# Dilated attention computed two heads at a time on halves of TensorE's array, with projection blocks between the pairs

## The chip, the cores and the metric

The kernel runs on one core of a Trainium2 chip as one launch. The metric is device time in microseconds (us), the median of several runs; lower is better.

## The reference

The reference is a network of two blocks over 256 tokens of width 1024, in float32. The first block has a mixing layer with a recurrence, a gated FFN with a short convolution, a dilated attention layer with 16 heads of 64 features, and another FFN. The second block (with a modulation by a condition vector) has a block attention with 8 heads of 128 features, a gated FFN, a convolution layer and another FFN. The change concerns only the dilated attention:

```python
h = rmsnorm(x, od_norm[j])
qkv = (h @ od_w_qkv[j]).reshape(bsz, t_len, 3, C_HEADS, C_HEAD)
y = dilated_attention(qkv[:, :, 0], qkv[:, :, 1], qkv[:, :, 2])
x = x + y @ od_w_out[j]
```

`dilated_attention` runs a softmax for each of the patterns (window, dilation) = (128, 1), (512, 4), (2048, 16) and weighs the three results by their log-sum-exp. That equals one softmax over all causal keys in which a key counts as often as patterns hold it; both kernels compute it so, with log(count) added to the scores.

## The kernel before

Everything stays in SBUF; only weights stream in. A projection weight comes as chunks of 2 MB in a ring of two slots, by DMAs that SyncE (SP) issues. Each chunk is used in halves of 128 x 2048. For each half ACT writes a rounded high part (`split_hi`, line 564, tile `whi`), DVE writes the rest (`split_lo`, line 570, tile `wlo`), and PE makes three products (hi x hi, hi x lo, lo x hi) per tile. Four buffers hold the parts, and each engine's `w.go()` makes the parts three halves ahead of the one that is used. Each engine's program is written out by hand, and its instructions run in that order; they meet by semaphores. A PSUM bank's semaphore counts how often the bank was read out; `opened(e, key)` waits until the previous user of the bank has been read, and `read_out(key)` names the count at which this one has. `bank_plan` fixes which bank each product uses.

The stage of the change, in order:
- `pe_tile` makes Q and K in eight tiles (`("qkv", i, q)`, lines 993 to 995), with features on the partitions; ACT copies each tile out (line 1420). Two pairs of products of the modulation (`adahi`, `adalo`, `one_r`) stand ahead of tile 7 and behind it.
- Then a loop over i = 0 to 18. In step i PE makes the scores of head i (two products, lines 2389 and 2390: queries 0 to 127 against 128 keys, queries 128 to 255 against 256 keys), turns the exponentials of head i - 2 (three transposes, line 2373), and multiplies head i - 3 with V (lines 2405 to 2407, P as the stationary operand, 64 columns of V moving, the result with tokens on the partitions). `pe_rows` (lines 1008 to 1010) makes V in four halves within steps 0, 1, 3 and 4.
- DVE adds the bias and takes maxima (lines 1865, 1869) and copies three of four turned heads out (1877); ACT takes the exponentials (1444) and copies every fourth (1453).
- After each eight heads DVE inverts the sums and scales the result into `xn` (`od_scaled`, lines 1836 and 1841), PE turns it with eight transposes (`od_turned`, line 2382), and ACT and DVE write its high and low parts (`yhi` line 1436, `ylo` line 1849).
- `pe_sum_rows` multiplies with `od_w_out` in four blocks (line 1022, 24 products of 512 columns each); in the last two blocks the second half of the tokens waits until the first half's sums are done, so that the next norm can begin (its turn is line 759).

Elsewhere in the kernel, the first mixing layer already has float32 products on halves of the array: line 2213 (64 rows, halves alternating) and line 2292 (64 columns of the stationary operand, halves alternating). The second block's attention already scales P on DVE (line 1940) and writes its result with features on the partitions (1521 on ACT, 1947 on DVE).

Of the kernel before, what the change touches and what calls it, by code (L numbers as in the profile page):

```python
# [7 lines left out]
F32 = mybir.dt.float32  # L8
U32 = mybir.dt.uint32
F32R = mybir.dt.float32r  # L10
ALU = mybir.AluOpType
# [107 lines left out]
MOD_Q = {0: 0, 1: 1, 3: 2, 4: 3}  # L119

# [139 lines left out]
def bank_plan():  # L260
# [69 lines left out]
    for m in range(8):  # L330
        for n in ADA["qkv"]["sums", ("tile", m)]:
            P.use(("ada", n), r())
        for j in behind_norm(m):
            P.use(("qkv", j // 2, j % 2), r())
    for n in ADA["qkv"]["sums", "end"]:
        P.use(("ada", n), r())
# [11 lines left out]
    def od_between(i):  # L348
        if i in (0, 3):
            P.use(("v", "qkv", i // 3, 0), 4)  # L350
            P.use(("v", "qkv", i // 3, 1), 5)
        if i == 12:
            P.use(("yt", 0, 0), r())
            P.use(("yt", 0, 1), r())

    def od_values(h):
        if h % 8 == 0:
            for n in range(2):
                P.use(("o", n, h // 8), (6, 4)[h // 8] + n)

    attention("od", 16, od_between, od_values)
    sums("od_out", (2, 3, 6, 7))
    r = Ring((0, 1))
    P.use(("yt", 1, 0), r())
    P.use(("yt", 1, 1), r())
# [39 lines left out]
def program(nc, A, consts, out):  # L405
    with ExitStack() as ctx:
# [300 lines left out]
        YTOK = XN  # L707
        od_sums, od_rl = (ATT[:, 32 * i:32 * i + 32].rearrange("p (h n) -> p h n", n=2) for i in (1, 2))
# [510 lines left out]
        def scalar_program(e):  # L1219
# [193 lines left out]
            for i in range(4):  # L1413
                for q in range(2):
                    split_hi(e, w.go())
                    if i == q == 0:
                        act_first(e, 2)
                    e.wait_ge(*block_done(("qkv", i), q))
                    j = 4 * (i % 2) + 2 * q
                    e.activation((QT if i < 2 else KT)[:, j:j + 2, :], c3(ps_of(("qkv", i, q))[:, :], 2),  # L1420
                                 ACT.Copy).then_inc(bank_sem(("qkv", i, q)), 1)
                    act_ada_parts(e, ADA["qkv"]["parts", ("tile", 2 * i + q)], 2)

            def v_piece(name, i, q):
                split_hi(e, w.go())
                if q:
                    e.wait_ge(*used_up((name, 4 + i), 1))
                    e.wait_ge(S["ada_acc"], 4 * ADA["qkv"]["range"][1])
                    for n in range(2):
                        key = ("v", name, i, n)  # L1430
                        e.activation(VV[:, n, 512 * i:512 * i + 512], ps_of(key)[:, :], ACT.Copy).then_inc(bank_sem(key), 1)

            def od_turned(q):
                for n in range(2):
                    e.wait_ge(S["yt_turned"], 2 * q + n + 1)
                    e.activation(YT[0][:, 4 * q:4 * q + 4, 128 * n:128 * n + 128],
                                 c3(ps_of(("yt", q, n))[:, :], 4), ACT.Copy).then_inc(S["od_hi"], 1)
# [17 lines left out]
            for i in range(19):  # L1455
                if i < 16:
                    exp(i, "od", 16, 0, None)
                if i in (0, 1, 3, 4):
                    v_piece("qkv", i // 3, i % 3)
                if i == 12:  # L1460
                    od_turned(0)
                if 2 <= i < 18:
                    turned(i - 2, "od", 0)
            act_load_root(e)
            split_hi(e, w.go())
            od_turned(1)
            for i in range(3):
                split_hi(e, w.go(AHEAD * (i < 2)))
# [42 lines left out]
            for i in range(11):  # L1511
                if i < 8:
                    exp(i, "mo", 8, 32, None)
                if i < 2:
                    v_piece("qkv2", 1, i)
                if 2 <= i < 10:
                    turned(i - 2, "mo", 16)
                if i >= 3:
                    h = i - 3
                    e.wait_ge(S["at_values"], 16 + h + 1)  # L1520
# [92 lines left out]
        def vector_program(e):  # L1613
# [211 lines left out]
            for m in range(8):  # L1825
# [5 lines left out]
            dve_ada_sums(e, ADA["qkv"]["sums", "end"])  # L1831

            def od_scaled(q):
                r = od_rl[:, 8 * q:8 * q + 8, :]
                e.wait_ge(S["at_exp"], 8 * q + 8)
                e.reciprocal(r, od_sums[:, 8 * q:8 * q + 8, :]).then_inc(S["od_inverse"], 1)
                e.wait_ge(S["od_inverse"], q + 1)
                e.wait_ge(S["at_values"], 8 * q + 8)
                for n in range(2):
                    key = ("o", n, q)  # L1840
                    e.tensor_tensor(c3(YTOK[:, n, 512 * q:512 * q + 512], 8), c3(ps_of(key)[:, :], 8),
                                    bc(r[:, :, n], 64), ALU.mult).then_inc(bank_sem(key), 1)

            def od_turned(q):
                for n in range(2):
                    key = ("yt", q, n)
                    hi, lo = (y[:, 4 * q:4 * q + 4, 128 * n:128 * n + 128] for y in YT)
                    e.wait_ge(S["od_hi"], 2 * q + n + 1)
# [30 lines left out]
            for i in range(19):  # L1879
                if i < 16:  # L1880
                    scores(i, "od", 16, 0)
# [683 lines left out]
```

## Time and profile before

| | |
|---|---|
| median of 3 runs | 1342.65 us (1340.93 to 1343.02) |
| profiled execution | 1340.58 us |
| its span | 1338.8 us |
| PE busy | 1283.9 us, 96% |
| DVE busy | 962.9 us, 72% |
| ACT busy | 705.4 us, 53% |
| stage of the change | 431 to 527 us from the span's start |

PE is TensorE's matmul side, PEld its weight loads, DVE is VectorE, ACT ScalarE. A matmul's duration includes its pipeline, so the time that it costs PE is the distance from one start to the next. In the chain of work, each piece has only the time that it adds. "PEclk" is the granted clock, 1.00 for 2.4 GHz and 0.50 for 1.2 GHz.

### The profile page before, as it was taken

Reading aid. Unit: us, or ns where it says so; the run is one execution under the profiler, and the core shown is the slowest. Engines: PE = TensorE matmul, PEld = TensorE weight load, DVE = VectorE, ACT = ScalarE, POOL = GpSimd, SP = SyncE. Lnnn points to the kernel's source line nnn. Section 1 sums busy time; section 2 is a strip of 40 time slices with the busy share of each in tenths; the row PEclk is TensorE's granted clock in tenths of the full one; section 3 lists DMA queues with packets and bytes.
Section 4 is the critical chain, followed back from the end, with each engine's and each line's share of the span. In section 5 each row is a group of like instructions: output and inputs, shape, how many; then the busy total and the mean of one; then the engine's idle time right before and its main releaser. Section 6 shows DMA issues by size and latency. Waiting matters only on the chain.

```text
span 1338.8 us, 24152 instructions
## 1 busy us (share of the span) xinstructions
PE 1283.9 (96%) x10267; PEld 1191.4 (89%) x10267; DVE 962.9 (72%) x1266; ACT 705.4 (53%) x1012; POOL 16.5 (1%) x26
## 2 busy tenths in 40 slices
PE   6988999999999999999999988999999999999998
PEld 5878879999989978999998986899999899899997
DVE  5775248888877565898887577699997676676543
ACT  5933348665565444766556544654434644644442
POOL 0002000000000000000000000000000000000000
PEclk9999899999999979999999998999999999999999
DMA  9450236877457504777743541599997355675551
GB/s 308 150 189 3 65 118 218 278 250 241 147 209 272 188 1 132 247 264 241 250 172 130 188 170 57 190 309 342 352 337 261 137 203 190 204 271 184 186 189 38
DMA packets 161572, 263.77 MB, mean 197 GB/s; under 512 B 3565, under 2 KB 95929, under 8 KB 161466
## 3 DMA queue, kind: packets, MB, share of 16 engines
q1 hardware_dynamic: 160586, 259.54, 56.1%
q10 hardware_dynamic: 880, 2.69, 0.6%
q8 instruction: 81, 1.33, 0.4%
q14 instruction: 25, 0.20, 0.0%
HBM read 261.17 MB, written 1.05 MB: 196 GB/s over the span
## 4 chain that ended last, share of the span: by engine, by line
PE 73%; DVE 14%; DMA 5%; ACT 5%; issue 3%; DVEq 0%; SPq 0%; ACTq 0%
PE ps L1022 19%; PE ps L993 12%; PE ps L995 12%; PE ps L994 12%; DVE wlo L570 4%; DVE acc L2026 3%; DMA arena<-in_w_ada_dram 3%; PE ps L2204 2%; ACT whi L564 1%; PE ps L779 1%; PE ps L781 1%; PE ps L780 1%; PE ps L759 1%; DVE arena L2008 1%; DMA ring<-in_ev_w_in_dram 1%
## 5 line engine op out<-in xcount | busy, mean ns | idle before, releaser
L570 DVE TENSOR_TENSOR wlo<-ring,whi 128x2048 fp32r<-128x2048 f32 x195 | 445.3, 2288 | 129.8 <-ACT whi L564 128.8
L993 PE MATMUL ps<-ghi,whi 128*128 128x256 f32 x1632 | 458.5, 281 | 0.0
L994 PE MATMUL ps<-glo,whi 128*128 128x256 f32 x1632 | 455.8, 279 | 0.0
L995 PE MATMUL ps<-ghi,wlo 128*128 128x256 f32 x1632 | 455.6, 279 | 0.0
L564 ACT ACTIVATE whi<-ring 128x2048 fp32r<-128x2048 f32 x195 | 372.2, 1914 | 104.1 <-PE ps L1022 70.0
L993 PEld LDWEIGHTS ps<-ghi,whi 128*128 128x128 f32 x1632 | 306.4, 188 | 1.2 <-issue 0.5
L994 PEld LDWEIGHTS ps<-glo,whi 128*128 128x128 f32 x1632 | 306.1, 188 | 1.2 <-issue 0.5
L995 PEld LDWEIGHTS ps<-ghi,wlo 128*128 128x128 f32 x1632 | 306.1, 188 | 0.0
L1022 PE MATMUL ps<-whi,yhi 128*128 128x512 f32 x480 | 160.1, 398 | 1.8 <-DVE ylo L1807 0.8
L1022 PE MATMUL ps<-wlo,yhi 128*128 128x512 f32 x480 | 156.9, 392 | 0.0
L1022 PE MATMUL ps<-whi,ylo 128*128 128x512 f32 x480 | 156.4, 391 | 0.0
L2026 DVE SCALAR_TENSOR_TENSOR acc<-arena,small,acc 128x512 f32<-128x512 f32 x168 | 126.2, 751 | 7.9 <-DMA arena<-in_w_ada_dram 2.7
L1022 PEld LDWEIGHTS ps<-whi,ylo 128*128 128x128 f32 x480 | 90.7, 189 | 19.4
L1022 PEld LDWEIGHTS ps<-wlo,yhi 128*128 128x128 f32 x480 | 90.9, 189 | 19.1
L1022 PEld LDWEIGHTS ps<-whi,yhi 128*128 128x128 f32 x480 | 89.1, 190 | 21.0 <-issue 2.2
L2068 DVE SCALAR_TENSOR_TENSOR arena<-arena,cols 128x254 f32<-128x254 f32 (+1 forms) x176 | 74.5, 479 | 20.8 <-ACT arena L1583 19.8
L779 PE MATMUL ps<-whi,ghi 128*128 128x256 f32 x224 | 63.5, 284 | 6.9 <-DVE glo L921 6.7
L2083 DVE TENSOR_TENSOR ylo<-arena,yhi 128x256 fp32r<-128x256 f32 x88 | 37.0, 421 | 45.0 <-ACT yhi L1600 44.8
L1581 ACT ACTIVATE arena<-ps 128x512 f32<-128x512 f32 x44 | 26.3, 597 | 73.6 <-PE ps L995 71.9
L780 PE MATMUL ps<-wlo,ghi 128*128 128x256 f32 x224 | 62.3, 278 | 0.0
L781 PE MATMUL ps<-whi,glo 128*128 128x256 f32 x224 | 62.3, 278 | 0.0
L1587 ACT ACTIVATE arena<-ps 128x256 f32<-128x256 f32 x44 | 16.7, 380 | 83.2 <-PE ps L995 83.1
(301 smaller groups left out, 1650.7 us busy)
## 6 DMA issues: line engine op xcount, KB each, us to landing
arena<-in_w_ada_dram SPq DMA_DIRECT2D x48, 1024.0 KB, 7.0
ring<-in_ff_w_up_dram SPq DMA_DIRECT2D x44, 1024.0 KB, 7.5
ring<-in_w_gate_up_dram SPq DMA_DIRECT2D x44, 1024.0 KB, 7.5
ring<-in_ff_w_down_dram SPq DMA_DIRECT2D x10, 2048.0 KB, 7.8
ring<-in_w_down_dram SPq DMA_DIRECT2D x10, 2048.0 KB, 7.8
ring<-in_od_w_qkv_dram SPq DMA_DIRECT2D x6, 2048.0 KB, 8.0
ring<-in_w_qkv_dram SPq DMA_DIRECT2D x6, 2048.0 KB, 8.2
ring<-in_w_in_dram SPq DMA_DIRECT2D x6, 2048.0 KB, 7.9
```

What stands on the lines that cost most here:

```text
L564: e.activation(shaped(WHI[i % NB], k), v, ACT.Copy).then_inc(S["w_hi"], 1)
L570: e.tensor_tensor(shaped(WLO[i % NB], k), v, shaped(WHI[i % NB], k).bitcast(F32), ALU.subtract).then_inc(S["w_lo"], 1)
L779: e.matmul(o, h[0][:, c, t], wh, start=c == 0, stop=False)
L780: e.matmul(o, h[0][:, c, t], wl, start=False, stop=False)
L781: x = e.matmul(o, h[1][:, c, t], wh, start=False, stop=c == NK - 1)
L993: e.matmul(o, wh, h[0][:, k, :], start=k == 0, stop=False)
L994: e.matmul(o, wh, h[1][:, k, :], start=False, stop=False)
L995: x = e.matmul(o, wl, h[0][:, k, :], start=False, stop=k == NK - 1)
L1022: x = e.matmul(ps[:, :], YT[l][:, src_k + i, t], w[r][:, i, 512 * h:512 * h + 512], start=first, stop=last)
L2026: e.scalar_tensor_tensor(a, AW[:, k, :], SC[:, k:k + 1], a, ALU.mult, ALU.add).then_inc(S["ada_acc"], 1)
L2068: e.scalar_tensor_tensor(t[a][:, lag:256], z[:, 256 * a:256 * a + 256 - lag], conv_col(f, 2 - lag, a * NF + p), t[a][:, lag:256], ALU.mult ...
L2083: e.tensor_tensor(YT[1][:, p % 8, :], tg[r], YT[0][:, p % 8, :].bitcast(F32), ALU.subtract).then_inc(S["y_lo"], 1)
```

## The change

Heads are handled in pairs p = 0 to 7, and a table `OD` gives one order that PE, ACT and DVE all follow.
- Scores of a pair: head 2p reads partitions 0 to 63, head 2p + 1 partitions 64 to 127, and the products alternate between the two; each head has a bank of its own.
- P is kept for four pairs (two of them in `xn`). DVE scales it by the inverse sums before the turn (`od_share`).
- Six transposes per pair. Both copies out of PSUM are ACT's.
- Values: V is now the stationary operand (64 columns), P the moving one (128 columns). The two heads write partitions 0 to 63 and 64 to 127 of one bank, so the result has features on the partitions; its turn is gone (`od_scaled`, `od_turned`). ACT writes its high part, DVE the low one.
- The first scores stand ahead of tile 7 (`"keys"`), the V halves and the four blocks of `od_out` stand between the pairs, and the banks go round differently.

The diff, cut to its core (the renumbered counts of the second attention, and the code that was removed in the order described above, are left out):

```diff
+OD = [("s", 0), ("keys", 7), ("s", 1), ("p", 0), ("v", 0), ("wh", 0), ("wl", 0),
+      ("t", 0), ("s", 2), ("p", 1),
+      ("v", 1), ("p", 2), ("t", 1), ("o", 0), ("wh", 1), ("s", 3), ("lo", 0), ("wl", 1),
+      ("t", 2), ("o", 1), ("s", 4), ("p", 3), ("lo", 1),
+      ("v", 2), ("t", 3), ("o", 2), ("wh", 2), ("s", 5), ("p", 4), ("lo", 2), ("wl", 2),
+      ("v", 3), ("t", 4), ("o", 3), ("wh", 3), ("s", 6), ("p", 5), ("lo", 3), ("wl", 3),
+      ("rows", 0), ("t", 5), ("o", 4), ("wh", 4), ("s", 7), ("p", 6), ("lo", 4), ("wl", 4),
+      ("rows", 2), ("p", 7), ("t", 6), ("o", 5), ("t", 7), ("lo", 5), ("o", 6), ("lo", 6), ("wh", 5), ("wl", 5),
+      ("rows", 4), ("o", 7), ("lo", 7), ("wh", 6), ("wl", 6), ("rows", 6)]
 # bank_plan
+    for what, i in OD:
+        if (what, i) == ("s", 0):
+            r = Ring(range(6))
+        if (what, i) == ("t", 4):
+            r = Ring(range(4))
...
+        elif what == "s":
+            P.use(("od", "s", 2 * i), r())
+            P.use(("od", "s", 2 * i + 1), r())
+        elif what == "v" and i % 2 == 0:
+            P.use(("v", "qkv", i // 2, 0), 6)
+            P.use(("v", "qkv", i // 2, 1), 7)
+        elif what == "t":
+            P.use(("od", "t", 2 * i), r())
+            P.use(("od", "t", 2 * i + 1), r())
+        elif what == "o":
+            P.use(("od", "o", i), r())
+        elif what == "rows" and i == 0:
+            sums("od_out")
 # ACT
+            for what, p in OD:
+                if what == "keys":
+                    qk_tile(p)
+                elif what == "s":
+                    for n, c in enumerate(KEYS):
+                        for g in range(2):
+                            h, t = 2 * p + g, pairs[p % 4][:, g, c]
+                            e.wait_ge(S["at_max"], 2 * p + n + 1)
+                            x = e.activation(t, t, ACT.Exp, bias=nmx[:, h, n:n + 1], accum_out=sums[:, h, n:n + 1])
+                    x.then_inc(S["at_exp"], 1)
...
+                elif what == "v" and p % 2:
+                    v_out("qkv", p // 2)
+                elif what == "wh":
+                    split_hi(e, w.go())
+                elif what == "t":
+                    for g in range(2):
+                        key = ("od", "t", 2 * p + g)
+                        e.wait_ge(S["at_turned"], p + 1)
+                        if p >= 2:
+                            e.wait_ge(S["at_values"], p - 1)
+                        e.activation(pts[2 * (p % 2) + g], ps_of(key)[:, 0:384], ACT.Copy).then_inc(bank_sem(key), 1)
+                elif what == "o":
+                    e.wait_ge(S["at_values"], p + 1)
+                    e.activation(YT[0][:, p, :], ps_of(("od", "o", p))[:, 0:256], ACT.Copy).then_inc(S["od_hi"], 1)
 # DVE
+            def od_lo(p):
+                key = ("od", "o", p)
+                e.wait_ge(S["od_hi"], p + 1)
+                e.tensor_tensor(YT[1][:, p, :], ps_of(key)[:, 0:256], YT[0][:, p, :].bitcast(F32),
+                                ALU.subtract).then_inc(bank_sem(key), 1)
+            def od_share(p):
+                two, t = slice(2 * p, 2 * p + 2), pairs[p % 4]
+                e.wait_ge(S["at_exp"], p + 1)
+                e.reciprocal(rl[:, two, :], sums[:, two, :]).then_inc(S["od_inverse"], 1)
+                e.wait_ge(S["od_inverse"], p + 1)
+                for g in range(2):
+                    for n, c in enumerate(KEYS):
+                        x = e.tensor_scalar(t[:, g, c], t[:, g, c], rl[:, 2 * p + g, n:n + 1], None, ALU.mult)
+                x.then_inc(S["od_p"], 1)
...
+                elif what == "s":
+                    e.wait_ge(S["at_scores"], p + 1)
...
+                    for g in range(2):
+                        key = ("od", "s", 2 * p + g)
+                        e.scalar_tensor_tensor(t[:, g, :], ps_of(key)[:, 0:384], 0.125, CT[:, C_BOD:C_BOD + 384], ALU.mult,
+                                               ALU.add).then_inc(bank_sem(key), 1)
...
+                    for n, c in enumerate(KEYS):
+                        e.tensor_reduce(nmx[:, two, n], t[:, :, c], AX, ALU.max, negate=True).then_inc(S["at_max"], 1)
 # PE
+                elif what == "s":
+                    ps = [opened(e, ("od", "s", 2 * p + g)) for g in range(2)]
...
+                    for g in range(2):
+                        e.matmul(ps[g][:, 0:128], QT[half[g], p, 0:128], KT[half[g], p, 0:128], start=True, stop=True)
+                    for g in range(2):
+                        x = e.matmul(ps[g][:, 128:384], QT[half[g], p, 128:256], KT[half[g], p, 0:256], start=True, stop=True)
+                    x.then_inc(S["at_scores"], 1)
+                elif what == "v":
+                    pe_rows(e, w, lambda n: ("v", "qkv", p // 2, n), 2, p % 2)
+                elif what == "t":
+                    ps = [opened(e, ("od", "t", 2 * p + g)) for g in range(2)]
+                    e.wait_ge(S["od_p"], p + 1)
+                    for g in range(2):
+                        for i in range(3):
+                            c = slice(128 * i, 128 * i + 128)
+                            x = e.transpose(ps[g][:, c], pairs[p % 4][:, g, c], ident)
+                    x.then_inc(S["at_turned"], 1)
+                elif what == "o":
+                    ps = opened(e, ("od", "o", p))
...
+                    for n, c, start, stop in ((0, 0, True, True), (0, 1, True, False), (1, 2, False, True)):
+                        t = slice(128 * min(c, 1), 128 * min(c, 1) + 128)
+                        for g in range(2):
+                            v = slice(128 * p + 64 * g, 128 * p + 64 * g + 64)
+                            x = e.matmul(ps[half[g], t], VV[:, n, v], pts[2 * (p % 2) + g][:, 128 * c:128 * c + 128],
+                                         start=start, stop=stop)
+                    x.then_inc(S["at_values"], 1)
+                elif what == "rows":
+                    pe_sum_rows(e, w, "od_out", p, p, NK, kept, [read_out(("od", "o", k)) for k in (p, p + 1)])
```

On PE, in the middle of the heads, the kernel before has this order: the scores of a head, the turn of another and the values of a third follow each other with nothing between (`arena` holds Q, K, V and P; `consts_sb` the identity; `x3` is three in a row).

```order
L2389 MATMUL ps<-arena 128x128
L2390 MATMUL ps<-arena 128x256
L2373 MATMUL ps<-consts_sb,arena 128x128 x3
L2405 MATMUL ps<-arena 128x64
L2406 MATMUL ps<-arena 128x64
L2407 MATMUL ps<-arena 128x64
L2389 MATMUL ps<-arena 128x128
L2390 MATMUL ps<-arena 128x256
```

In the changed kernel, behind V half 1, two pairs' blocks and the scores of pair 4 stand like this, with V half 2 (`L1028`) behind them. Line 2444 is the turn, 2455 the values, 2432 and 2434 the scores.

```order
L2444 MATMUL ps<-consts_sb,arena 128x128 x6
L2455 MATMUL ps<-arena 64x128 x6
L2432 MATMUL ps<-arena 128x128 x2
L2434 MATMUL ps<-arena 128x256 x2
L2444 MATMUL ps<-consts_sb,xn 128x128 x6
L2455 MATMUL ps<-arena 64x128 x6
L2432 MATMUL ps<-arena 128x128 x2
L2434 MATMUL ps<-arena 128x256 x2
L1028 MATMUL ps<-whi,ghi 128x256
```

So a block of a pair has 6 transposes, 6 products for the values and 4 for the scores, and the 64 in the values' rows is now on the stationary side. This is the one place where two such blocks follow each other ahead of a V half; elsewhere each stands alone between V halves or `od_out` blocks.

On DVE, at the end of the stage, the changed kernel has the scaling of pair 7, two low parts, a weight half, the last low part, and the last weight half; the norm (`L1092`) follows.

```order
L1908 RECIPROCAL att<-att 128x4
L1912 TENSOR_SCALAR xn<-xn,att 128x128
L1912 TENSOR_SCALAR xn<-xn,att 128x256
L1912 TENSOR_SCALAR xn<-xn,att 128x128
L1912 TENSOR_SCALAR xn<-xn,att 128x256
L1901 TENSOR_TENSOR ylo<-ps,yhi 128x256 x2
L589 TENSOR_TENSOR wlo<-ring,whi 128x2048
L1901 TENSOR_TENSOR ylo<-ps,yhi 128x256
L589 TENSOR_TENSOR wlo<-ring,whi 128x2048
L1092 TENSOR_TENSOR x<-x,ps 128x512 x2
```

The low part of pair 7 (`lo 7`), for which block 6 of `od_out` waits on PE, has a weight half ahead of it in DVE's queue.

## Rows read from the trace of the kernel before

**Rows 1.** The page, engines: busy us, share of the span, instructions.

```profile
PE 1283.9 (96%) x10267; PEld 1191.4 (89%) x10267; DVE 962.9 (72%) x1266; ACT 705.4 (53%) x1012; POOL 16.5 (1%) x26
```

**Rows 2.** Windows: stretch, length, engines' busy us (instructions), PEclk, DMA, GB/s.

```profile
437.00:480.00 43.00, 42.78 (x321) 37.26 (x319) 26.21 (x46) 22.81 (x56) 0.00 (x0) 1.00 0.37 136
480.00:488.00 8.00, 6.19 (x43) 4.66 (x41) 6.37 (x14) 3.01 (x11) 0.00 (x0) 1.00 0.00 0
488.00:508.00 20.00, 20.00 (x78) 16.99 (x78) 8.19 (x16) 7.11 (x17) 0.00 (x0) 0.57 0.13 39
```

**Rows 3.** Chain that ended last, 431 to 527 us: start, us added, what.

```profile
431.23 0.24 PE ps L2496
...
437.40 0.61 ACT arena L1420
...
439.28 0.12 PE ps L1009
...
444.62 0.41 PE ps L2389 x2
...
473.40 0.41 PE ps L2389 x2
473.82 0.43 PE ps L2390 x2
474.25 0.48 PE ps L2373 x3
474.73 0.17 PE ps L2405 x2
...
475.35 0.41 PE ps L2389 x2
...
484.30 0.98 ACT arena L1444 x4
...
500.75 7.69 PE ps L1022 x24
508.44 0.87 PE ps L2382 x8
509.31 10.94 PE ps L1022 x48
...
523.16 1.06 PE ps L759 x8
524.22 2.75 PE ps L1022 x12
```

**Rows 4.** First mixing layer: PE's timeline at two places, and weight loads of line 2292.

```profile
115.64 1.16 PE L2213 MATMUL ps<-mix 64*128 64x128 f32 x16
116.73 2.96 PE L2204 MATMUL ps<-pre 64*64 64x64 f32 x94
...
170.71 1.09 PE L2292 MATMUL ps<-mix 128*64 128x128 f32 x16
171.63 1.04 PE L2292 MATMUL ps<-pre 128*64 128x128 f32 x16
...
L2292 PEld LDWEIGHTS ps<-mix x32: 132/137/137, 170.7 to 175.3; 128*64 128x64 f32 x32
```

**Rows 5.** DVE and ACT: timeline pieces (start, us), then groups (busy, mean ns).

```profile
472.34 0.56 DVE L1865 SCALAR_TENSOR_TENSOR arena<-ps,consts_sb 128x384 f32<-128x384 f32 x1 [0.48 <-PE ps L2390]
472.94 0.61 DVE L1869 TENSOR_REDUCE att<-arena 128x1 f32<-128x128 f32 x2
...
803.89 0.55 DVE L1940 TENSOR_SCALAR arena<-arena,att 128x128 f32<-128x128 f32 x2
824.87 0.42 DVE L1947 TENSOR_TENSOR ylo<-ps,yhi 128x256 fp32r<-128x256 f32 x1 [1.74 <-ACT yhi L1521]
...
L570 DVE TENSOR_TENSOR wlo<-ring,whi 128x2048 fp32r<-128x2048 f32 x5 | 11.5, 2291 | 10.2 <-ACT whi L564 10.2
L564 ACT ACTIVATE whi<-ring 128x2048 fp32r<-128x2048 f32 x5 | 9.5, 1901 | 0.0
```

More of the change, by code:

```diff
@@ L329, in bank_plan, with qkv_tile @@
     norm(2, r, True)
-    for m in range(8):
+    def qkv_tile(m):
         for n in ADA["qkv"]["sums", ("tile", m)]:
@@ L334, in bank_plan @@
             P.use(("qkv", j // 2, j % 2), r())
[L335 to L336 removed]
+    for m in range(7):
+        qkv_tile(m)
+    for what, i in OD:
[4 more added lines that the diff above has]
+        if what == "keys":
+            qkv_tile(i)
+            for n in ADA["qkv"]["sums", "end"]:
+                P.use(("ada", n), r())
+        elif what == "s":
[11 more added lines that the diff above has]
+            sums("od_out")
     def attention(name, heads, between, values):
@@ L1426, in v_piece @@
                 if q:
[L1427 to L1437, printed above, removed]
+                    v_out(name, i)
             def exp(h, name, heads, at, last):
@@ L1830, in vector_program @@
                 dve_ada_parts(e, ADA["qkv"]["parts", ("tile", m)])
[L1831 to L1848, printed above, removed]
-                    e.tensor_tensor(lo, c3(ps_of(key)[:, :], 4), hi.bitcast(F32), ALU.subtract).then_inc(bank_sem(key), 1)
+            for m in range(7):
+                qk_tile(m)
             def scores(h, name, heads, at):
@@ new lines, in vector_program @@
+            for what, p in OD:
+                two, t = slice(2 * p, 2 * p + 2), pairs[p % 4]
+                if what == "keys":
+                    qk_tile(p)
+                    dve_ada_sums(e, ADA["qkv"]["sums", "end"])
+                elif what == "s":
+                    e.wait_ge(S["at_scores"], p + 1)
+                    e.wait_ge(S["ada_acc"], 4 * ADA["qkv"]["range"][1])
+                    if p >= 4:
+                        e.wait_ge(S["at_turned"], p - 3)
+                    for g in range(2):
[3 more added lines that the diff above has]
+                    for g in range(2):
+                        e.wait_ge(*read_out(("od", "s", 2 * p + g)))
+                    for n, c in enumerate(KEYS):
+                        e.tensor_reduce(nmx[:, two, n], t[:, :, c], AX, ALU.max, negate=True).then_inc(S["at_max"], 1)
+                elif what == "p":
+                    od_share(p)
+                elif what == "lo":
+                    od_lo(p)
+                elif what == "wl":
+                    split_lo(e, w.go())
```

168 lines of the change are left out of this document (53 added, 115 removed).

## The prediction

> **What bounds the kernel now.** I read four views of the profile in this order. The page first: the tensor engine (PE) is busy for 96% of the span [rows 1], so only what shortens PE's own queue, or the stretches where it waits or runs slowly, is worth anything. Then the windows over the stage that is edited [rows 2]: up to 480 us PE is never idle for long and its granted clock reads 1.00; from 480 to 488 it is busy for 6.19 of 8.00 us; from 488 to 508 it is "busy" throughout, at a granted clock of 0.57, mostly the lower level (1.2 GHz) where the rest runs at 2.4. Then the chain that ended last, in order of time [rows 3]. It is PE through almost all of the stage, with one detour over DVE and ACT near 484.30. Last the neighbouring stage that already works on halves of the array [rows 4], and the durations of the other engines' operations [rows 5].
>
> The stage to follow begins at 431.23, after projection tile 6, and ends at 524.22 + 2.75 = 526.97, after the last product of `od_out` [rows 3]: 95.7 us. Its parts at the full clock, so that every later term has a counterpart:
> - tile 7 with two pairs of sums: 431.23 to 437.40, and 0.47 for the second pair of sums, 6.6;
> - four V halves: 439.28 to 444.62 is 5.34 for 47 of the 48 products, so 5.45 each, 21.8;
> - `od_out`: 96 products at 10.94 / 48 = 0.228, 21.9;
> - the turn of the next norm: 1.06 and about 0.1 of waiting, 1.2;
> - sixteen heads: 473.40 to 475.35 is 1.95 each (scores 0.41 + 0.43, turn 0.48, values about 0.62), 31.2;
> - two turns of the result, 0.87 at 508.44 and about as much for the other, 1.9.
> Together 84.6 [rows 3]. The other 11.1 us: 8.8 are the lower clock (487.60 to 500.75 is PE's own work at half speed, so about 6.6, and the 24 products at 500.75 took 7.69 where 24 x 0.228 = 5.5, so 2.2); the remaining 2.3 are waits around 480 to 488, where PE waits for the scaled and turned first half of the result.
>
> **The change part by part.**
> *Removed.* The two scale-and-turn blocks with their 16 transposes (1.9), and the waits they cause (2.3). DVE scales P before the turn, so no head waits for eight heads' inverses. The work that let the clock fall goes with it: between 480 and 488 PE had only small products with gaps, and the fall came at 488 [rows 2]. In the new order each short block stands between products of 5.5 us. I take back the whole 8.8, with a doubt below.
>
> *Products in pairs.* PE gets 20 instructions for scores and values per pair, first head on one half of the array, second on the other, alternately. No row of this stage has that, but two of the earlier stage do [rows 4]. 64-row stationaries on alternating halves: 16 instructions of 128 columns from 115.64 to 116.73, 68 ns each. 64-column stationaries, 128 columns moving, alternating halves, exactly the new form of the values: 16 instructions from 170.71 to 171.63, 57 ns each. Serial, the same 128 columns cost 107 ns (half of the 0.43 / 2 that 256 columns take at 473.82 [rows 3]). So:
> - values: 12 x 0.057 = 0.69, where two heads cost 1.24;
> - scores: 4 x 0.068 = 0.27 for the 128-column ones. The 256-column ones are 4 instructions of 0.215. The two of one head follow each other and only the second overlaps the other head's first, so I take 3 x 0.215 minus what runs beside the neighbours, and 0.85 for the scores in all. Bounds: 0.70 with perfect overlap, 1.68 with none (two heads now);
> - turns: 6 transposes at 0.87 / 8 = 0.11, so 0.65 (three take 0.48 now with the passage before them);
> - each passage between full array, row halves and column halves: the 128 columns at 473.40 (line 2389) cost 0.41 where two times 0.107 are the arithmetic [rows 3], so 0.2 per passage. With three beyond what is in the prices above, 0.55 per pair.
> A pair is 0.85 + 0.65 + 0.69 + 0.55 = 2.75, eight are 22.0 against 31.2. Bounds: 2.3, and 4.0 (no overlap), that is 18.4 to 32.
>
> On these passages the Trainium skill speaks against the change: "TensorEngine Tiling (Array Packing)", section "Key Properties", says that a change of tiling mode drains the engine, and "TensorE: Matmul & The Clock Gate", section on the mechanism of row and column tiling, says that weight loads overlap running matmuls only where the row group differs, which the two column halves do not. By the trace the first costs some 0.2 us; the second, taken literally, is a rival below, and the 57 ns of rows 4 disagree with it.
>
> *Moved to other engines.* Per pair DVE has two 0.56 (bias), two reductions over both heads (I bound them by the four small ones, 2 x 0.61), an inverse (0.2), four multiplications (2 x 0.55) and one subtraction (0.42) [rows 5]: 4.1, minus overlaps. Eight pairs are 32 and eight weight halves at 2.29 are 18, some 50. ACT has 4 exps (2 x 0.98 [rows 3]), two copies (about 1.0), one high part (about 0.4), so 8 x 3.4, and 8 x 1.90 for the weights: 42. PE's sum below is 78, so neither is the bound on average. What can hurt is latency: from the scores of a pair to its turn are 1.0 (bias), 0.45 (first reduction), 1.8 (exps) and 1.2 (inverse, scale), with handovers 4.7 us; one V half or one row block (5.45) covers that where it stands between.
>
> *Where PE will wait.* I walked the four queues pair by pair with these prices.
> - Scores 0 stand right behind tile 6 and reuse its bank, so they wait for ACT's copy (0.61 at 437.40 [rows 3]): 0.9.
> - Values 0 need the copy of V that ACT makes only after the second V half, with a turn of 0.65 in between: 0.65.
> - Scores 4 reuse the bank of values 0, which DVE reads in `lo 0`, queued behind the bias and maxima of scores 3: 1.0.
> - Scores 6 reuse a bank of turn 4, behind ACT's copy of V: 0.3. Turn 7 waits for DVE's scale of pair 7, behind a weight half of 2.29: 0.3.
> - Rows 6 wait for `lo 7`. On ACT the high part of values 7 comes behind `wh 5`, and on DVE `lo 7` stands behind `wl 5`, which itself waits for `wh 5`. Values 6 end about 3.5 us before values 7; ACT and DVE then have 0.4 + 1.9 + 2.3, so `lo 7` ends 1.7 after values 7.
> Sum 5.0. The rest of SP's queue is as before: the same loads in the same order, each released by the same subtraction, and DMA moved 39 GB/s or less through 480 to 508 [rows 2], so no load is late.
>
> *The sum.* 6.6 + 21.8 + 21.9 + 1.2 + 22.0 + 5.0 = 78.5 against 95.7: 17.2 us. Behind the stage PE is bound again and the stages are hung on its products, so I carry the gain whole to the end. The profiled execution took 1340.58 us for a span of 1338.8; it would be 1323.4 (span 1321.6). The median of the runs shown is 1342.65, 2.07 above it, so the prediction is 1342.65 - 17.2 = 1325.4, given as 1325.5.
>
> **The rivals.**
> - *No overlap in the halves*: pairs cost 4.0 as two heads do now, 32 in place of 22. The gain is 7.2, 1335.4. For: alternation by instruction, not within one. Against: rows 4. Chance 0.10.
> - *The clock falls in the new order too*: the stretch from turn 1 to scores 4 is 6.6 us of short blocks with 1.65 of waiting, and at the end turn 6 to rows 6 is similar. That is 75% busy; 480 to 488 was 77% and was followed by the fall [rows 2]. Each fall costs at least 3 us, since the dense products from 500.75 ran at the lower level too for some 4.4 us (2.2 lost at half speed). One fall: gain 14; two with longer waits: gain 9, 1333.5. Chance of 0.25 that it is more than one fall or that waits are twice mine (another 5.0, gain 12, 1330.5).
> - *Weight loads of the column halves exposed*: a 64-column load takes 137 ns [rows 4]. Twelve instructions at 0.107 + 0.137 are 2.93 for 0.69 + passages: about 2.1 per pair more, 16.8 in all. Gain 0.4, 1342.3. Against: 57 ns per instruction in the same form. Chance 0.02. (This is what the rule on weight loads of the Trainium skill's page "TensorE: Matmul & The Clock Gate" would have here.)
> - *Slower*: the loads are exposed in both kinds. The scores' eight instructions then pay 137 ns each too, 1.3 to 1.5 per pair more, 12 in all: 16.8 + 12 - 17.2 = 11.6 slower, 1354. It decides from 17.2 / 160 = 108 ns more per instruction than rows 4 have. A drain per alternation would look the same. Against: both rows in rows 4. Chance 0.03.
> - My forecast, gain 12 to 23: 0.60.
>
> **How the numbers follow.** A fifth of a per cent, about 2.7 us, is what a measurement of this kernel can tell from no change. Faster by more are the forecast, the first two rivals: 0.94 to 0.95. Within it the third, 0.02; slower 0.03, and 0.01 for what I do not see. The range for 8 in 10: the low end is pairs at 2.3 (3.6 more) and half the waits (2.5), with some gain where the norm behind overlaps, 1318; the high end takes in the clock's rival at 1333.5, so 1334.
>
> **What the profile of the changed kernel would show.** Right: a stretch of 78 to 79 us from tile 6's end to the last `od_out` product; scores of a pair near 0.85 to 1.05 and values near 0.7 from start to next start; granted clock 1.00 in all windows of the stage; PE's idle time near 5 us, with the longest wait before rows 6, released by DVE's `ylo`. Wrong: 20 instructions per pair at 107 ns or more; a window of 0.5 to 0.6 clock after scores 4 or around turn 7; PE waiting at turns for DVE's scaling, which would mean that a chain of 4.7 us is longer than the block over it; or the next FFN starting with a wait for weights, giving the gain back.

## The result, and the profile after

The changed kernel takes 1325.47 us (median of four runs, 1323.73 to 1326.37) against 1341.79 for the kernel before (1340.91 to 1343.02, four runs beside it): ratio 0.9883 [0.9864, 0.9903], 16.3 us less. The profiled execution has a span of 1323.7 us. One run of the first experiment below took 4502 us; it is counted in no figure here.

The page after, engines (as [rows 1]). PE has 18.9 busy microseconds less and still 96% of the span, so it is still the bound; ACT and DVE are where they were.

```profile
PE 1265.0 (96%) x10251; PEld 1175.6 (89%) x10251; DVE 960.9 (73%) x1276; ACT 709.6 (54%) x1028; POOL 16.6 (1%) x26
```

Windows over the edited stage after (as [rows 2]). What to see is the column behind the last "(x0)": the granted clock is 1.00, the upper level, in every one of them, also where PE is busy for only 8.78 or 8.71 of 10 us.

```profile
431.00:440.00 9.00, 8.31 (x69) 7.69 (x68) 7.00 (x10) 5.19 (x12) 0.00 (x0) 1.00 0.48 167
440.00:450.00 10.00, 9.76 (x82) 8.39 (x81) 6.82 (x12) 5.88 (x13) 0.00 (x0) 1.00 0.19 75
450.00:460.00 10.00, 8.78 (x85) 7.49 (x83) 7.88 (x20) 6.56 (x18) 0.00 (x0) 1.00 0.58 211
...
480.00:490.00 10.00, 10.00 (x60) 7.94 (x60) 7.65 (x16) 6.84 (x17) 0.00 (x0) 1.00 0.25 81
490.00:500.00 10.00, 8.71 (x69) 6.70 (x68) 5.67 (x10) 6.64 (x11) 0.00 (x0) 1.00 0.64 211
```

The chain that ended last, after (as [rows 3]). The stage begins at 432.09, where tile 6 is done and ACT copies it, and ends at 506.81 + 2.77 = 509.58. One pair's block between V halves is 466.75 to 469.06: turn (line 2444), values (2455), scores (2432 and 2434). From 498.10 to 505.74 the chain leaves PE: it goes over ACT's last weight half, DVE's, and the norm.

```profile
432.12 0.61 ACT arena L1441
...
466.75 0.66 PE ps L2444 x6
467.40 0.81 PE ps L2455 x12
468.21 0.42 PE ps L2432 x4
468.63 0.43 PE ps L2434 x4
469.06 0.32 PE ps L1028
...
485.26 5.69 PE ps L1042 x24
...
496.97 0.83 PE ps L2455 x12
...
498.10 1.91 ACT whi L583
...
500.04 2.29 DVE wlo L589
...
502.33 0.61 DVE x L1092
...
505.74 1.06 PE ps L779 x8
506.81 2.77 PE ps L1042 x12
```

PE's waits in the stage after, by what released them: total us, times, longest.

```profile
PE ps L1042 <- DVE ylo L1901: 1.3, 1, 1.3
PE ps L779 <- DVE xn L965: 1.0, 1, 1.0
PE ps L2432 <- DVE ylo L1901: 1.0, 1, 1.0
PE ps L2432 <- ACT arena L1441: 0.7, 1, 0.7
PE ps L2455 <- ACT arena L1453: 0.3, 1, 0.3
PE ps L2444 <- DVE arena L1912: 0.2, 1, 0.2
```

The stage now takes 509.58 - 432.09 = 77.5 us where it took 95.7. Term by term: the pairs cost 20.2 us (worked out below) in place of 31.2, which is 11.0 less; the two turns of the result (1.9), the lower clock (8.8) and the waits of before (2.3) are gone; and 5.8 come back as waits (3.5, and 0.9 more at the norm) and a rest of 1.4. That is 18.2.

Since DVE's norms stand on both sides of it in every kernel here, the experiments are measured between two of their instructions: from the reciprocal of the second half of the norm ahead of the stage to that of the first half of the norm behind it. Before, these are 392.11, in DVE's timeline:

```profile
392.11 0.17 DVE L888 RECIPROCAL small<-small 128x1 f32<-128x1 f32 x1 [0.36 <-ACT small L880]
```

and 522.33, in the chain, 130.22 us apart (after: 392.56 and 504.91, 112.35 apart).

```profile
522.33 0.17 DVE small L888
```

So 17.9 us are gained from norm to norm, and 16.3 in the medians. What lies behind the second norm took 816.5 us before and 818.8 after, with the same code; over the kernels below it lies between 816.1 and 820.7. A single span therefore says little below some 4 us; the interval from norm to norm says more. It comes from one profiled execution of each kernel.

### The profile page after: what moved, and what is told of

The parts are those of the page before. It is cut to its first block, busy times and chain, and to the rows that moved or that the text cites. A ratio compares the mean times of both kernels' runs of the same rounds, so it can differ in the third digit from the quotient of the medians.

```text
span 1323.7 us, 24151 instructions
## 1 busy us (share of the span) xinstructions
PE 1265.0 (96%) x10251; PEld 1175.6 (89%) x10251; DVE 960.9 (73%) x1276; ACT 709.6 (54%) x1028; POOL 16.6 (1%) x26
## 4 chain that ended last, share of the span: by engine, by line
PE 71%; DVE 14%; ACT 5%; DMA 5%; issue 4%; DVEq 0%; SPq 0%; ACTq 0%
PE ps L1042 19%; PE ps L1013 12%; PE ps L1014 12%; PE ps L1015 12%; DVE wlo L589 4%; DVE acc L2071 3%; DMA arena<-in_w_ada_dram 3%; PE ps L2249 2%; ACT whi L583 2%; PE ps L799 1%; PE ps L801 1%; PE ps L800 1%; PE ps L779 1%; DVE arena L2053 1%; DMA ring<-in_ev_w_in_dram 1%
```

## The experiments

None of them leaves out or changes any arithmetic; they move instructions, waits or banks. "Norm to norm" is the stretch just defined (130.2 before, 112.35 after). The four kernels of the first group were timed against 1339.84 for the kernel before, the others against 1340.29.

### Scores head by head

```diff
 for g in range(2):
     e.matmul(ps[g][:, 0:128], QT[half[g], p, 0:128], KT[half[g], p, 0:128], start=True, stop=True)
-for g in range(2):
     x = e.matmul(ps[g][:, 128:384], QT[half[g], p, 128:256], KT[half[g], p, 0:256], start=True, stop=True)
```

> The changed kernel, but PE makes all four score instructions of a pair's first head and then all four of the second, in place of alternating between the halves of the array. Theory (instructions on different halves run beside each other): only the last of head one overlaps the first of head two, so a pair's scores cost about 1.3 to 1.4 us in place of the 0.85 that the chain of the changed kernel shows; eight pairs are 4 us, stage 77.5 -> 81.5, time 1325.5 -> 1329.5. Rival (the halves bring nothing by overlap, the gain is fewer passages between array shapes): scores stay at 0.85, time within 1 us of 1325.5.

1327.00 us (1325.80 to 1331.75, three runs), ratio 0.9906 [0.9872, 0.9941], a wide interval; norm to norm 112.43, the same as the changed kernel. The chain of this kernel at the same block (2433 is now the line of the 256-column products):

```profile
469.90 0.43 PE ps L2432 x4
470.33 0.43 PE ps L2433 x4
```

My expectation missed: the scores cost 0.86 as before. That is the number of the rival, and the time is 1.5 us above the changed kernel's, near its "within 1 us"; but its reason, that the halves bring nothing by overlap, doesn't follow. In program order the four groups stand as: first head 128 columns, first head 256, second head 128, second head 256, each two instructions. Two windows of this kernel within the block (PE busy, PEld busy, clock, DMA), first of line 2432 alone:

```profile
469.95:470.00 0.05, 0.05 (x2) 0.05 (x4) 1.00 0.00 0
470.10:470.15 0.05, 0.05 (x4) 0.04 (x2) 1.00 0.00 0
```

and the same windows of line 2433 alone:

```profile
469.95:470.00 0.05, 0.00 (x0) 0.00 (x0) 1.00 0.00 0
470.10:470.15 0.05, 0.00 (x0) 0.05 (x2) 1.00 0.00 0
```

By 470.15 all four products of line 2432, the second head's too, have started, and none of line 2433, though the first head's product of line 2433 stands ahead of the second head's of line 2432 in the program. In the trace the first two of them start 14 ns apart; two instructions of one head's product stand 0.21 us apart where the heads run in turn (below), so these two are of different heads. By the records PE takes the other half's instructions ahead of their turn, so what is said above, that each engine's instructions run in the order of its program, isn't so here. The Trainium skill, page "TensorE: Matmul & The Clock Gate", section "The mechanism", says that matmuls start and end in program order; the records of this block show otherwise. The records could be off, but the unchanged 0.86 agrees with them. It also means that the order within a block of scores doesn't matter, so this kernel could not test the overlap. The fourth one below (the two heads in turn) does.

### Values head by head

```diff
-for n, c, start, stop in ((0, 0, True, True), (0, 1, True, False), (1, 2, False, True)):
-    t = slice(128 * min(c, 1), 128 * min(c, 1) + 128)
-    for g in range(2):
+for g in range(2):
+    for n, c, start, stop in ((0, 0, True, True), (0, 1, True, False), (1, 2, False, True)):
+        t = slice(128 * min(c, 1), 128 * min(c, 1) + 128)
```

> The changed kernel, but the six value instructions of a pair's first head come before the six of the second. Theory (overlap between column halves): 12 instructions cost 1.2 us in place of 0.81, eight pairs +3.2 us, time about 1328.7. Rival (weight loads of column halves are the limit, so alternation is worth nothing): values stay at 0.81, time within 1 us of 1325.5. A second rival: with a head's instructions in a row the loads are no better hidden, and they cost 0.24 each, 2.9 us a pair, time about 1342.

1328.05 us (1326.81 to 1329.59, four runs), ratio 0.9906 [0.9881, 0.9930], norm to norm 113.95, 1.6 us more. In its chain the values of a pair cost:

```profile
468.82 1.07 PE ps L2455 x12
```

That is 0.26 more than 0.81, and eight times this is 2.1; PE's waits in the stage are 0.4 shorter (4.1 against 4.5), which leaves about the 1.6. I had expected 1.2 and 3.2 more in all, so the order costs half of what I thought; the rivals (0.81 unchanged, or 2.9) are out. A serial block would take more (1.7, below). So with column halves too the two heads overlap partly where they stand one behind the other, six instructions apart, and the alternating order is worth 1.6 us from norm to norm over the head-by-head one.

### The blocks of `od_out` not spread

All four blocks stand behind the last pair.

```diff
-      ("rows", 0), ("t", 5), ("o", 4), ("wh", 4), ("s", 7), ("p", 6), ("lo", 4), ("wl", 4),
-      ("rows", 2), ("p", 7), ("t", 6), ("o", 5), ("t", 7), ("lo", 5), ("o", 6), ("lo", 6), ("wh", 5), ("wl", 5),
-      ("rows", 4), ("o", 7), ("lo", 7), ("wh", 6), ("wl", 6), ("rows", 6)]
+      ("t", 5), ("o", 4), ("wh", 4), ("s", 7), ("p", 6), ("lo", 4), ("wl", 4),
+      ("p", 7), ("t", 6), ("o", 5), ("t", 7), ("lo", 5), ("o", 6), ("lo", 6), ("o", 7), ("lo", 7),
+      ("rows", 0), ("wh", 5), ("wl", 5), ("rows", 2), ("rows", 4), ("wh", 6), ("wl", 6), ("rows", 6)]
```

> The changed kernel with all four blocks of the output projection behind the last pair, where the kernel before had them; V halves, pairs, halves of the array and the DVE scaling stay. Theory (the spread blocks cover the chain from scores to turn, 4.7 us, and keep the clock up): PE waits at the turns of pairs 5, 6 and 7 for 2 to 5 us in all, and the granted clock falls to 0.5 at the end of the pairs and stays there for 4 to 6 us of dense products; together 4 to 10 us slower than the changed kernel, 1330 to 1336. Rival (pairs and the missing turn of the result bring the gain by themselves): no fall of the clock, less than 1.5 us slower.

1331.97 us (1328.81 to 1334.64, six runs), ratio 0.9935 [0.9913, 0.9958]; norm to norm 120.58, 8.2 us more than the changed kernel. Its windows (as [rows 2]):

```profile
480.00:482.00 2.00, 2.00 (x20) 1.50 (x19) 1.82 (x1) 1.03 (x3) 0.00 (x0) 0.70 0.58 183
482.00:490.00 8.00, 4.26 (x26) 2.95 (x26) 6.40 (x15) 6.24 (x14) 0.00 (x0) 0.50 0.00 1
490.00:492.00 2.00, 1.62 (x16) 1.36 (x16) 0.78 (x3) 0.75 (x2) 0.00 (x0) 0.74 0.77 220
492.00:512.00 20.00, 19.64 (x101) 16.12 (x98) 6.94 (x7) 6.55 (x11) 0.00 (x0) 1.00 0.34 108
```

and two turns in PE's timeline, with the idle time before them and what ended it:

```profile
479.72 0.85 PE L2444 MATMUL ps<-consts_sb,arena 128*128 128x128 f32 x6 [3.73 <-DVE ylo L1901]
...
487.12 1.51 PE L2444 MATMUL ps<-consts_sb,xn 128*128 128x128 f32 x6 [3.74 <-DVE ylo L1901]
488.57 1.55 PE L2455 MATMUL ps<-arena 128*64 128x128 f32 x12
```

Both prices of not spreading are there. PE waits 3.7 us twice at a turn, from the end of a pair's scores over DVE's bias and maxima, ACT's exponentials and DVE's scaling; the last 0.3 us of it is a low part in DVE's queue behind the scaling (`ylo`), whose bank the turn takes. And the granted clock falls to 0.50, the lower level, behind the first gap, so that twelve value products take 1.55 in place of 0.88. It is 1.00 again from 492, ahead of the long row of `od_out` products, which starts at 493.63.

The waits are the larger part: PE's waits in the stage sum to 10.7 us where the changed kernel has 4.5, so 6.2 of the 8.2 are waits and some 2.0 are left for the clock and the changed passages. I had expected 2 to 5 us of waits at the turns (7.9 were measured) and 4 to 6 us of dense products at the lower clock; the stretch at the lower clock, 480.8 to 491.0, held the last pairs and their gaps, and no dense product. The total of 8.2 was in the range.

### The two heads in turn

Here PE waits for the first head's last product before it starts the second head's, in scores and in values.

```diff
 for g in range(2):
+    if g:
+        x.then_inc(S["first_scores"], 1)
+        e.wait_ge(S["first_scores"], p + 1)
     e.matmul(ps[g][:, 0:128], QT[half[g], p, 0:128], KT[half[g], p, 0:128], start=True, stop=True)
-for g in range(2):
     x = e.matmul(ps[g][:, 128:384], QT[half[g], p, 128:256], KT[half[g], p, 0:256], start=True, stop=True)
...
-for n, c, start, stop in ((0, 0, True, True), (0, 1, True, False), (1, 2, False, True)):
-    t = slice(128 * min(c, 1), 128 * min(c, 1) + 128)
-    for g in range(2):
+for g in range(2):
+    if g:
+        x.then_inc(S["first_values"], 1)
+        e.wait_ge(S["first_values"], p + 1)
+    for n, c, start, stop in ((0, 0, True, True), (0, 1, True, False), (1, 2, False, True)):
+        t = slice(128 * min(c, 1), 128 * min(c, 1) + 128)
```

> The changed kernel, but within a pair's scores and within its values PE starts the second head only when the first head's last product is done (a wait of PE on its own semaphore, which adds a drain of 0.1 to 0.3 us each time). In the two runs before, the order by head alone left the scores at 0.86 us, because the two halves still ran beside each other, and raised the values from 0.81 to 1.07. Theory (the halves' gain is overlap): scores 0.85 -> 1.5 to 1.8, values 0.81 -> 1.4 to 1.7, together 1.2 to 1.8 us a pair, from norm to norm 10 to 14 us more than the changed kernel's 112.4, time 1335 to 1340. Rival (the gain is fewer passages between array shapes): only the two drains come on top, at most 0.5 us a pair, 4 us in all, under 1330.

1337.70 us (1335.73 to 1340.62, ten runs), ratio 0.9974 [0.9961, 0.9986]; norm to norm 126.98, 14.6 us more, where 10 to 14 were expected and the rival has 4 at most. Most of the gain is gone. The chain at one block (2460 values, 2435 and 2436 scores):

```profile
474.69 0.81 PE ps L2460 x6
475.55 0.87 PE ps L2460 x6
476.42 0.42 PE ps L2435 x2
476.83 0.45 PE ps L2436 x2
477.33 0.48 PE ps L2435 x2
477.81 0.43 PE ps L2436 x2
```

By the starts in the trace, one head's six value products here take 0.60 us from the first start to the last, and in the changed kernel both heads' twelve take the same 0.60; one head's scores take 0.54 here, both heads' 0.55 there. So in both kinds the two halves ran wholly beside each other. Values are 1.73 from first start to the scores, scores 1.83: 3.56 where the changed kernel has 0.81 + 0.85 = 1.66. Eight times 1.9 is 15.2.

Not all of this is overlap. Within a head's values the products are 0.109 us apart, and 0.330 across the wait. The second head's own products are 6 x 0.109 for the values and 2 x 0.109 + 2 x 0.219 for the scores, together 1.3; the other 0.6 of a pair is what the two waits and the fresh starts behind them cost. So overlap is worth about 8 x 1.3 = 10.4 us, an estimate from these starts, and the waits that the experiment adds 4 to 5. PE's other waits in the stage are 1.0 shorter (3.5 against 4.5).

The granted clock also fell once here, behind the first scores:

```profile
431.00:435.00 4.00, 3.25 (x21) 2.36 (x20) 3.93 (x4) 0.60 (x1) 0.00 (x0) 1.00 0.19 70
435.00:440.00 5.00, 5.00 (x28) 4.75 (x28) 3.26 (x7) 2.87 (x7) 0.00 (x0) 0.66 0.71 242
```

That is up to 5 x 0.34 = 1.7 us of the 14.6. The changed kernel has the same gap of 0.69 us there and nearly the same busy time, and its clock stayed:

```profile
431.00:435.00 4.00, 3.31 (x27) 2.69 (x26) 3.77 (x4) 1.12 (x2) 0.00 (x0) 1.00 0.09 33
```

What decided between the two isn't shown by any run here.

### The last values ahead of the last weight halves

```diff
-      ("rows", 2), ("p", 7), ("t", 6), ("o", 5), ("t", 7), ("lo", 5), ("o", 6), ("lo", 6), ("wh", 5), ("wl", 5),
-      ("rows", 4), ("o", 7), ("lo", 7), ("wh", 6), ("wl", 6), ("rows", 6)]
+      ("rows", 2), ("p", 7), ("t", 6), ("o", 5), ("t", 7), ("lo", 5), ("o", 6), ("lo", 6), ("o", 7), ("lo", 7),
+      ("wh", 5), ("wl", 5), ("rows", 4), ("wh", 6), ("wl", 6), ("rows", 6)]
```

> The changed kernel with the last pair's values ahead of output block 4 on PE, and its high and low part ahead of the weight half on ACT and DVE. Theory (the wait before the last output block is lo 7 behind a weight half of 1.90 + 2.29 us): that wait of 1.3 to 1.5 us is gone and nothing takes its place but 0.1 to 0.3 at the values of pair 7, which follow the copies of its turn; stage 1.2 us shorter, time about 1324.3. Rival (the norm's chain behind the block sets the end anyway): stage unchanged.

1323.45 us (1322.35 to 1323.58, four runs), ratio 0.9869 [0.9846, 0.9892]; norm to norm 111.64, 0.7 less than the changed kernel, where 1.2 were expected. The wait of 1.3 ahead of block 6 is gone, but the chain shows what takes its place: both weight halves now stand together on DVE, ahead of the sums for which the norm waits.

```profile
495.51 1.92 ACT whi L583
...
497.45 4.49 DVE wlo L589 x2
...
501.94 0.61 DVE x L1092
```

The wait at the norm's turn has grown from 1.0 to 1.8 us, and values 7 now wait 0.4 for their copies:

```profile
PE ps L779 <- DVE xn L965: 1.8, 1, 1.8
```

In all PE waits 4.4 us where it waited 4.5. So the 0.7 isn't waiting saved; that values 7 no longer stand alone between dense blocks, with a passage on either side, may be the reason, which no run here tests.

### Two early waits, the end's weight halves, and both

The first kernel moves the low part of pair 0 ahead of the scores of pair 3 on DVE and starts the round of banks elsewhere, so that scores 0 don't take tile 6's bank. The second puts the weight halves 4 and 5 one place earlier each, and the last values ahead of block 4. The third has both.

```diff
-      ("v", 1), ("p", 2), ("t", 1), ("o", 0), ("wh", 1), ("s", 3), ("lo", 0), ("wl", 1),
+      ("v", 1), ("p", 2), ("t", 1), ("o", 0), ("lo", 0), ("wh", 1), ("s", 3), ("wl", 1),
...
-            r = Ring(range(6))
+            r = Ring((4, 5, 0, 1, 2, 3))
```

```diff
-      ("v", 3), ("t", 4), ("o", 3), ("wh", 3), ("s", 6), ("p", 5), ("lo", 3), ("wl", 3),
-      ("rows", 0), ("t", 5), ("o", 4), ("wh", 4), ("s", 7), ("p", 6), ("lo", 4), ("wl", 4),
-      ("rows", 2), ("p", 7), ("t", 6), ("o", 5), ("t", 7), ("lo", 5), ("o", 6), ("lo", 6), ("wh", 5), ("wl", 5),
-      ("rows", 4), ("o", 7), ("lo", 7), ("wh", 6), ("wl", 6), ("rows", 6)]
+      ("v", 3), ("t", 4), ("o", 3), ("wh", 3), ("s", 6), ("p", 5), ("lo", 3), ("wl", 3), ("wh", 4), ("wl", 4),
+      ("rows", 0), ("t", 5), ("o", 4), ("wh", 5), ("s", 7), ("p", 6), ("lo", 4), ("wl", 5),
+      ("rows", 2), ("p", 7), ("t", 6), ("o", 5), ("t", 7), ("lo", 5), ("o", 6), ("lo", 6), ("o", 7), ("lo", 7),
+      ("rows", 4), ("wh", 6), ("wl", 6), ("rows", 6)]
```

> The changed kernel with the low part of pair 0 ahead of the bias of pair 3 on DVE, and with the banks taken in another rotation, so that the first scores don't follow tile 6 in its bank. Theory (both waits are what the walk through the queues said): the wait of 1.0 us before scores 4 and the 0.7 us before scores 0 are gone, norm to norm 112.4 -> 110.8 (1.6 less). Rival (in the rotation another reuse takes their place, or the end of the stage is set by DVE's queue, so that what is saved early comes back late): less than 0.8 us saved, with a longer wait elsewhere.

> The changed kernel with weight halves 4 and 5 prepared one pair earlier on ACT and DVE, and the last values and their parts ahead of output block 4. The run with only the last values early saved 0.7 us, since DVE then had two weight halves (4.49 us) ahead of the norm. Theory (the end of the stage is set by the weight halves in DVE's queue, not by PE): the wait before the last block and DVE's late start of the residual are both gone, norm to norm 112.4 -> 110.9 (1.5 less). Rival (the weight halves brought forward delay the chains of pairs 6 and 7): waits of 0.5 us or more at turns 5 to 7, nothing saved.

> Both edits together. Theory: the savings add up, norm to norm 112.4 -> 109.3, 3.1 us less than the changed kernel, time about 1322.4. Rival (one wait covers the other): 1.6 us less at most, about 1324.

| | time, us | norm to norm | against 112.35 |
|---|---|---|---|
| two early waits | 1326.68 (one run) | 110.47 | -1.9 |
| weight halves | 1320.49 (one run) | 110.48 | -1.9 |
| both | 1319.95 (1319.24 to 1322.12, five runs) | 108.99 | -3.4 |

Expected were -1.6, -1.5 and -3.1, so each hit, slightly low, and the two savings nearly add up. The first one's single time isn't lower than the changed kernel's although its stage is 1.9 us shorter: what lies behind the second norm took 820.7 us there against 818.8. Of this stretch 17 us ran at the lower granted clock, where it was 10 in the changed kernel and 3.4 in the kernel with both edits, so the time of the latter owes something to the clock outside the stage. With both, the ratio is 0.9847 [0.9826, 0.9867], the fastest version here. PE's waits that are left in it:

```profile
PE ps L2444 <- DVE arena L1912: 0.5, 1, 0.5
PE ps L2455 <- ACT arena L1500: 0.4, 1, 0.4
PE ps L2455 <- ACT arena L1453: 0.3, 1, 0.3
PE ps L779 <- DVE xn L965: 0.2, 1, 0.2
```

They sum to 1.4 where the changed kernel has 4.5, 3.1 less for 3.4 us won. In its chain PE's products reach up to the sums ahead of the norm, with no weight half between:

```profile
493.61 5.68 PE ps L1042 x24
...
499.31 0.70 DVE x L1092
```

## Why the prediction was right

It gave 1325.5 us and 78.5 for the stage; measured were 1325.47 and 77.5. That the time agrees to 0.03 us is luck. The stage gained 18.2 where 17.2 were forecast, and the spans of the two profiled executions differ by 15.1 only, so what lies outside the stage took some 3 us more after the change. And the forecast started from a median of 1342.65 of three runs, where four runs give 1341.79. What holds is the mechanism: the stage came out within 1 us, from terms of which none missed by more than 1.8.

- **Products in pairs, right.** Overlap within the pair carries the largest part of the gain: forced in turn, the two heads cost 14.6 us from norm to norm, of which about 10.4 are overlap by the starts in the trace, the rest the added waits and up to 1.7 a fall of the clock. The rival without overlap had them cost 10 more and a gain of 7.2; the kernel that realises it gains only 3.2 from norm to norm, since waiting for the first head costs more than a mere row of instructions.
- **The price of a pair, 0.23 us too high.** A block costs 0.66 + 0.81 + 0.85 and 0.2 for the passage to the V product behind (0.32 where 0.12 is the rule): 2.52 against 2.75. The scores' 0.85 and the turns' 0.65 came within 0.01. Values with the passage ahead of them are 0.81. I had 0.69 for the products and 0.55 for three passages; two show up in a block, about 0.15 into the values (the trace has the six pairs of products 0.109 apart, 0.65 in all) and 0.2 back to the full array, and the one into the scores is in their 0.85. Eight pairs are 20.2, 1.8 below the sum.
- **Scores, right total with a wrong reason.** I took the 256-column products to overlap in part, because two of one head follow each other. Four take 0.43 in the chain, as two do before [rows 3]: they overlap wholly. The 128-column ones take 0.42, passage included. In the changed kernel the products alternate in the program too, so no two of one head follow each other. The first experiment shows that even that order wouldn't matter: by the records PE takes the other half's instructions ahead.
- **The weight loads of column halves, right to trust the row.** Twelve products and a passage take 0.81, so at most 67 ns each, and the rivals with exposed loads of 137 ns [rows 4] are out. The Trainium skill's rule in "TensorE: Matmul & The Clock Gate", section "The mechanism", that loads overlap running matmuls only where the row group differs, would have given 2.9 us per pair for the values, by the prediction's estimate. This trace disagrees for the two column halves, by a factor of more than three. It disagrees for the whole array too: the V halves' weight loads take 0.188 us each while the products stand 0.12 apart. The same section also lets a load go ahead into a background weight buffer, and taken so it forecasts no exposed load.
- **The clock, right, with a part that may be luck.** 1.00 throughout. That spreading matters for it isn't just argued: with the four blocks behind the last pair it reads 0.50 from 482 to 490 us. But at the start of the stage, near 435, the same gap at nearly the same busy time was followed by a fall in the kernel with the heads in turn and by none in the changed one, so that no fall came there isn't explained. Not spreading costs 8.2 us, some 6.2 of them waits, nearly half of the 17.9.
- **Waits, 5.0 predicted, 4.5 measured, but not all in the same places.** (The terms listed in the prediction add up to 4.85.) Scores 0: 0.9 and 0.7. Values 0: 0.65 and 0.3. Scores 4: 1.0 and 1.0. Rows 6: 1.7 and 1.3, the longest and released by `ylo`, as said. Scores 6 and turn 7, 0.3 each, don't occur; turn 0, which I had without a wait, has 0.2. One of 1.0 was missing: the turn of the next norm (line 779), for which I had kept the 0.1 of before. I had followed DVE's queue to the low part that block 6 needs and not past it: behind `lo 7` comes the last weight half and only then the sum that the norm needs (500.04 and 502.33 in the chain). The kernel with the last values early, which removes the wait of rows 6, gets 0.7 in place of 1.3, as PE then waits 1.8 at that next place. No load came late, as said, but the 39 GB/s of [rows 2] is a mean over 20 us; within it, from 504 to 508, 192 were moved.
- **The rest of the stage.** 6.6 + 21.8 + 21.9 + 1.2 + 20.2 + 3.5, and 0.9 more at the norm, are 76.1; 1.4 of the 77.5 remain. Of these, 0.3 stand ahead of turn 1, which starts 0.40 us behind the last product of V half 1 where the turn behind V half 2 has 0.12. The rest are probably the passages that blocks standing alone pay again (scores 0, scores 1, turn 0 with scores 2), which I haven't measured by themselves.
- **The gain carried to the end, right as far as the runs can tell.** It is 17.9 from norm to norm and 16.3 in the medians. The difference of 1.6 is within what the stretch behind the norm varies by from kernel to kernel (816.1 to 820.7), so whether the change itself costs anything there isn't settled by these runs.

The two experiments don't split the gain: they lose 14.6 and 8.2, together more than the 17.9 gained. The first contains the waits that it adds itself, and the second brings a stretch at the lower clock of its own. No kernel here keeps the pairs with the old turn of the result, so its 1.9 us and the 2.3 of waiting around it rest on the trace of before alone.

## What to carry to other kernels

Small products that use half the array are best issued in pairs for both halves, and a row of another stage with the same shapes is a good price for them; here the price of a pair was right within 10%, where one rule taken by itself was off by a factor of three. Short blocks with a chain over DVE and ACT between them belong between long dense blocks: here that hid most of the chain's latency (6.2 us) and spared the stage a stretch at the lower clock. When walking an engine's queue for one wait, go on to the next consumer: removing a wait of 1.3 us gave 0.7, and 1.9 once the weight halves behind it were moved as well.

## What the runs showed of the hardware

- Products on different halves of the array's rows run side by side even when one head's stand wholly ahead of the other's: 0.85 us per pair alternating, 0.86 head by head, and 1.83 only when a wait forces them apart. From the first start to the last, one head alone takes 0.54 and both together 0.55. The records show all 128-column products of the second head starting by 470.15, before any 256-column product of the first, which stands ahead of them.
- Column halves run wholly side by side when they alternate (0.60 us from the first start to the last for both heads, and 0.60 for one of them alone), in part head by head; a pair's values cost 0.81, 1.07 head by head and 1.73 forced apart.
- The weight loads of column halves, 0.137 us each, hide behind products of at most 0.067 us each.
- A gap alone doesn't lower the granted clock: the wait of 1.3 us within 490 to 500 left it at 1.00, and the first of the gaps of 3.7 was followed by 0.50. A gap of 0.69 was followed by 0.66 over 5 us in one kernel (busy 3.25 of 4.00 us ahead of it) and by 1.00 in another (3.31 of 4.00).
